# Gathering pass 0 of a mixture-of-experts stage straight from the fp32 residual

## The reference

```python
x = x + gt1[:, None, :] * (merged @ w_o[l])
h2 = modulate(rmsnorm(x, norm2_g[l]), sh2, sc2)
x = x + gt2[:, None, :] * hier_moe(h2, rg_w[l], rg_b[l], re_w[l], re_b[l], exp_w1[l], exp_w3[l], exp_w2[l])
...
(jax.nn.silu(xblk @ w1[e]) * (xblk @ w3[e])) @ w2[e]
```

## Time and profile before

| | |
|---|---|
| median of 3 runs | 1790.93 us (1787.37 to 1791.93) |
| profiled execution, its own time | 1790.77 us |
| its span, first to last instruction | 1789.0 us |
| PE busy | 1741.2 us (97%) |
| DVE, ACT busy | 892.9 us, 393.7 us |
| read from HBM | 639 MB |

### The profile page before, as it was taken

How to read it: one execution, slowest core, us unless ns; L and a number is a source line. 1 busy time by engine, 2 the same in 40 slices (tenths; PEclk the granted TensorE clock), 3 DMA queues, 4 the chain that set the end, 5 groups by cost and what they waited for, 6 DMA issues and landing times.

```text
span 1789.0 us, 25919 instructions
## 1 busy us (share of the span) xinstructions
PE 1741.2 (97%) x10198; PEld 993.7 (56%) x10198; DVE 892.9 (50%) x1032; ACT 393.7 (22%) x480; POOL 0.8 (0%) x5
## 2 busy tenths in 40 slices
PE   4999999999999999999999999999999999999997
PEld 3888567777777776874434444444444444444442
DVE  5564959867778678555233323232323333333334
ACT  3001034433333233434111111110101010101011
POOL 0000000000000000000000000000000000000000
PEclk9999999999999999999999999999999999999999
DMA  9998539889879697654999999999999999999996
GB/s 368 387 379 323 188 142 344 331 310 353 331 290 363 244 371 305 238 201 188 408 422 422 422 422 422 422 422 422 422 422 422 422 422 422 422 422 422 422 422 272
DMA packets 137583, 641.95 MB, mean 359 GB/s; under 512 B 9155, under 2 KB 9283, under 8 KB 77251
## 3 DMA queue, kind: packets, MB, share of 16 engines
q1 hardware_dynamic: 137106, 639.18, 89.4%
q0 software_dynamic: 144, 1.70, 0.2%
q10 hardware_dynamic: 290, 0.46, 0.1%
HBM read 639.21 MB, written 2.10 MB: 358 GB/s over the span
## 4 chain that ended last, share of the span: by engine, by line
PE 78%; DMA 18%; DVE 2%; issue 1%; ACT 1%; SPq 0%; DVEq 0%; ACTq 0%
PE ps L951 18%; DMA ring<-in_exp_w 17%; PE ps L593 8%; PE ps L905 7%; PE ps L688 7%; PE ps L690 7%; PE ps L689 6%; PE ps L650 5%; PE ps L928 4%; PE ps L883 4%; PE ps L606 3%; PE ps L763 2%; PE ps L761 2%; PE ps L762 2%; DMA r_b<-in_ada_w 1%; PE ps L892 1%
## 5 line engine op out<-in xcount | busy, mean ns | idle before, releaser
L951 PE MATMUL ps<-ring 128*64 128x512 f32 x2048 | 466.3, 597 | 5.1 <-DMA ring<-in_exp_w 5.1
L951 PEld LDWEIGHTS ps<-ring 128*64 128x64 f32 x2048 | 143.3, 137 | 292.0 <-issue 291.9
L1729 DVE TENSOR_TENSOR r_h<-r_h,ps 128x1024 f32<-128x1024 f32 x124 | 146.0, 1218 | 204.4 <-PE ps L928 204.4
L689 PE MATMUL ps<-g_lo,h_hi 128*128 128x512 f32 x512 | 199.3, 389 | 0.0
L1702 DVE TENSOR_TENSOR r_c<-ps,scale 128x512 f32<-128x512 f32 x64 | 44.1, 689 | 284.0 <-PE ps L883 282.1
L1274 ACT ACTIVATE r_m<-ps 128x512 f32<-128x512 f32 x32 | 19.1, 597 | 698.6 <-PE ps L951 698.6
L688 PE MATMUL ps<-mix_hi,h_hi 128*128 128x512 f32 x384 | 156.6, 408 | 0.0
L1137 ACT ACTIVATE mix_hi<-ring 128x1024 fp32r<-128x1024 f32 x96 | 101.5, 1061 | 222.3 <-PE ps L690 222.3
L690 PE MATMUL ps<-mix_hi,h_lo 128*128 128x512 f32 x384 | 149.7, 390 | 0.0
L593 PE MATMUL ps<-r_h,ring 128*128 128x256 f32 x640 | 141.9, 385 | 1.3 <-ACT r_h L1083 1.3
L1455 DVE SCALAR_TENSOR_TENSOR r_m<-ring,col,r_m 128x2048 f32<-128x2048 f32 x53 | 124.4, 2347 | 30.3 <-DMA ring<-in_ada_w 30.1
(11 more groups left out here) (271 smaller groups left out, 1621.6 us busy)
## 6 DMA issues: line engine op xcount, KB each, us to landing
ring<-in_exp_w SPq DMA_DIRECT2D x320, 1024.0 KB, 19.9
ring<-in_ada_w SPq DMA_DIRECT2D x72, 1024.0 KB, 8.1
ring<-in_w_in SPq DMA_DIRECT2D x36, 2048.0 KB, 10.0
r_b<-in_exp_w SPq DMA_DIRECT2D x64, 1024.0 KB, 21.7
ring<-in_w_in SPq DMA_DIRECT2D x20, 1024.0 KB, 14.2
r_b<-in_ada_w SPq DMA_DIRECT2D x16, 1024.0 KB, 10.7
ring<-in_w_o SPq DMA_DIRECT2D x8, 2048.0 KB, 9.5
ring<-in_branch_w SPq DMA_DIRECT2D x6, 2048.0 KB, 8.6
```

The lines of the kernel that those rows point to most:

```text
L689: mm(ps[:, b + t, :], h, lo[:, cols], start=False, stop=False)
L951: last = mm(ps[m * NWIN:(m + 1) * NWIN, 2, :], xe[:, k, :], chunk(2 * c + m)[:, kk * F:(kk + 1) * F], start=(k == 0), stop=(k == KT - 1))
L1729: V.tensor_tensor(x1n, x1n, ps[:, (6, 4)[b]:(6, 4)[b] + 2, :].rearrange("p b n -> p (b n)"), ALU.add).then_inc(added, 1)
```

## The change

- **x1.** VectorE writes all eight blocks of x1 before it copies the four turned blocks. ScalarE squares two half tiles before its first copy. TensorE does all 32 transposes before the first logit product.
- **Gather of pass 0.** It reads x1 itself in fp32, with a selection `sel_r` that holds the root of each token's norm in place of a one. The selection is built by four operations on both tiles together. The bf16 selection `sel` is made in full after the tables.
- **Split of tile 1.** The pass 0 gather no longer needs it. Its first two quarters keep their place near the router. The other two and all four second rests are in pass 0, after the second half of the gather, and `gate2_row` waits for the low parts of tile 0. The gather for pass 1 goes from after chunk 1 to after chunk 3 of pass 0. ScalarE does two of tile 1's mid parts, then the exponentials, then waits for the gate row, and does the rest of the split behind it.
- **Small matmul pair.** The pair for the starts (L978, L979) goes ahead of the split of tile 1.
- **Head.** Piece 0 of `ada_w` comes as four transfers, one for each of its four rows, with a semaphore each.

```diff
             for n in range(4):
                 for t in range(TT):
                     turn_x1(n, t)
-                if n == 1:
-                    pe.wait_ge(rw_scaled, 1)
-                if n:
-                    for t in range(TT):
-                        logit_part(n - 1, t)
...
+            pe.wait_ge(rw_scaled, 1)
+            for n in range(4):
+                if n == 2:
+                    mm(ps[:, 5, 0:36], ones, cst_k[:, :], start=True, stop=False)
+                    mm(ps[:, 5, 0:36], ones[0:1, :], lrow[0:1, :], start=False, stop=True).then_inc(cst_done, 1)
+                for t in range(TT):
+                    logit_part(n, t)
...
-            first_rest(1, 0, 2)
             pe.wait_ge(cnt_ready, 1)
             mm(ps[:, 0, 128:160], ct[:, 0, :], tri[0:32, 0:32], start=True, stop=True).then_inc(start_done, 1)
-            first_rest(1, 1, 3)
...
             for b in range(2):
                 pe.wait_ge(lo_ready, b + 1)
-                first_rest(1, 2 + b, 4 + b)
-            for b in range(4):
-                second_rest(1, b, 2 + b)
+                first_rest(1, b, 4 + b)
...
                     if not with_second and c == 0:
                         gate2_row()
+                    if not with_second and c == 1:
+                        gather_x1(1)
+                        pe.wait_ge(gt2_saved, 1)
+                        first_rest(1, 2, 6)
+                        first_rest(1, 3, 7)
+                    if not with_second and c == 2:
+                        for b in range(4):
+                            second_rest(1, b, 4 + b)
...
-                    if c == 1 and not last_pass:
+                    if c == (1 if with_second else 3) and not last_pass:
+                        if not with_second:
+                            pe.wait_ge(lo_ready, 8)
...
-            pe.wait_ge(mid_ready, 8)
-            gather_parts((0, 1))
-            pe.wait_ge(lo_ready, 8)
-            gather_parts((2,)).then_inc(gathered, 1)
+            def gather_x1(half):
+                for kk in range(HALF):
+                    k = half * HALF + kk
+                    for t in range(TT):
+                        last = mm(gat[:, kk, :], x1_k[:, t, k // 4, k % 4, :], sel_r[:, t, :], start=(t == 0),
+                                  stop=(t == TT - 1))
+                last.then_inc(gathered, 1)
+            gather_x1(0)
...
-            pe.wait_ge(xe_ready, 1)
-            gather(1, sel)
...
-            one_hot(0, NWIN)
+            step(first_hot(0))
+            step(first_hot(1))
+            step(V.tensor_tensor(sel_r, sel_r, xs[:, 0:TT, :], ALU.add))
+            step(V.tensor_tensor(sel_r, sel_r, b8(stat[:, 6:8], NWIN), ALU.mult))
             v.sem_inc(all_sel, 1)
...
             for n in range(4):
-                save_x1(n, 0)
-                if n:
-                    save_turned(n - 1)
-                save_x1(n, 1)
-            save_turned(3)
+                for t in range(TT):
+                    save_x1(n, t)
+            for n in range(4):
+                save_turned(n)
```

More of the change, by code:

```diff
@@ L160, in build @@
         xs = r_c[:, 2176:2688].rearrange("p (c n) -> p c n", c=HALF)
+        sel_r = r_c[:, 2688:2816].rearrange("p (t n) -> p t n", t=TT)
         junk = r_m[:, 7168:8192]
@@ L180, in ada_count @@
         def ada_count(i):
-            return 32 * sum(j % ADA_FIRST == i % ADA_FIRST and j % 4 != 3 for j in range(i + 1))
+            return 32 * sum(j % ADA_FIRST == i % ADA_FIRST and j % 4 != 3 and j > 0 for j in range(i + 1))
         def head_w(i):
@@ L217, in build @@
         ada_in = [sem(f"ada_in{i}") for i in range(ADA_FIRST)]
+        ada_first = [sem(f"ada_first{i}") for i in range(4)]
         ada_last = [sem(f"ada_last{i}") for i in range(4)]
@@ L386, in load_head @@
                     sp.wait_ge(sq_done, 2)
-                if piece == 3:
+                if piece == 3 or i == 0:
                     for kk in range(4):
                         sp.dma_start(head_ada(i)[:, kk, :, :],
-                                     ada_v[:, 12 + kk, 0:2 * D].rearrange("p (v n) -> p v n", v=2)
-                                     [:, :, part * PART:(part + 1) * PART]).then_inc(ada_last[kk], 16)
+                                     ada_v[:, 4 * piece + kk, 0:2 * D].rearrange("p (v n) -> p v n", v=2)
+                                     [:, :, part * PART:(part + 1) * PART]
+                                     ).then_inc((ada_last if i else ada_first)[kk], 16)
                     return
@@ L934, in gate2_row @@
                 pe.wait_ge(diag2_ready, 1)
+                pe.wait_ge(lo_ready, 4)
                 for b in range(2):
@@ L1229, in _ @@
             A(stat[:, 20:21], keep[:, K_EPS:K_EPS + 1], ACT.Sqrt).then_inc(warm_up, 1)
+            square(0, 0)
+            square(1, 0)
             copy_turned(0)
-            square(0, 0)
             copy_turned(1)
-            square(1, 0)
+            square(0, 1)
             copy_turned(2)
-            square(0, 1)
+            square(1, 1)
+            copy_turned(3)
             root(0)
-            copy_turned(3)
-            square(1, 1)
             root(1)
@@ L1245, in _ @@
                 part_low(0, b, 4 + b)
[L1246 to L1249, removed]
+            for b in range(2):
+                part_mid(1, b, 4 + b)
             act.wait_ge(r_ask, 1)
@@ L1253, in _ @@
             A(rs[:, 8, :], rs[:, 7, :], ACT.Exp).then_inc(r_exp, 1)
+            act.wait_ge(gt2_row, 1)
+            A(gt2row, ps[:, 6:8, :], ACT.Copy).then_inc(gt2_saved, 1)
+            for b in range(2, 4):
+                part_mid(1, b, 4 + b)
+            for b in range(4):
+                part_low(1, b, 4 + b)
             act.wait_ge(table_ready, 1)
@@ L1356, in _ @@
                         v.wait_ge(ada_last[k - 12], 16 * (part + 1))
+                    elif i == 0:
+                        v.wait_ge(ada_first[k], 16)
                     elif k % 4 == 0:
@@ L1749, in _ @@
             v.sem_inc(table_ready, 1)
+            one_hot(0, PAIRS)
+            v.sem_inc(sel_full, 1)
             modulated(0, 1)
-            one_hot(NWIN, PAIRS)
-            v.sem_inc(sel_full, 1)
             v.wait_ge(r_exp, 2)
```

14 lines of the change are left out of this document (9 added, 5 removed).

## The result

The changed kernel takes 1801.74 us (median of 4 runs, 1800.54 to 1803.46), the kernel before 1790.54 us in as many runs beside it (1787.37 to 1791.93). The ratio is 1.0066, with a 95% interval of 1.0048 to 1.0083. So the change made the kernel **slower by 0.66%**, 11.2 us, where no measurable difference was forecast. The profiled execution took 1801.13 us.

A forecast was written before the change was run, and what follows sets the result against it. The DMA queue at 422 GB/s was taken to bound the loop; 7.5 us gained before pass 0, less 8.85 us added inside it, with a fresh queue start, left 0.3 us: 1790.5 us, range 1786.0 to 1794.0.

The forecast's parts named there:

- the price of the fp32 gather: Both pass 0 gathers: 0.114 us per instruction, 3.65 us each for 32; bounds 0.08 and 0.133.
- I take one fall, in one of the two: Ahead of chunk 0 of pass 0 or pass 1: one clock fall; none 1.3 us better, two 1.3 worse.
- Rival 3: From chunk 0 of pass 0: clock stays low through the pass, anchor 9 us back, 1799.8 us; chance 0.05.
- the anchor: Start of the unbroken weight stream, released by chunk 0 of pass 1: 861.15 us before, 860.8 forecast.
- The start price of 2.0 us: DMA queue starting from idle: full-rate stream begins 2.0 us behind the release.
- the sum: All terms: chunk 0 of pass 0 7.5 us earlier, pass 0 8.85 us longer, stream 0.3 us earlier, 1790.5 us.
- x1: Ahead of pass 0: logits ready 3.6 us earlier once VectorE no longer waits for TensorE.
- The wait ahead of the second gather of pass 1: In pass 1, the other half's gather waits for VectorE's modulation: 1.7 us added.
- The selection behind chunk 3: End of pass 0: ScalarE's copy of the next selection comes some 0.45 us after chunk 3.
- The head: Start of kernel: VectorE begins piece 0 1.0 us earlier but waits for piece 2; gain at most 0.16, taken as 0.
- Rival 2: Ahead of the passes: the 7.5 us gained survive, 1783.4 us; chance 0.10, plus 0.04 for a part.
- Rival 4: End of pass 0: selection or low parts arrive much later than chunk 3; 3 us more, 1793.9 us; chance 0.03.

The follow-up runs named there:

- gather_contiguous: Changed kernel, with pass 0's fp32 gather reading its 128 weight columns from a contiguous stretch of x1, not every fourth element: 1790.26 us, ratio 1.0002 to the kernel before.
- weight_step: Separate timing kernel that only copies x: groups of matmuls with weight elements 1, 2 or 4 apart; fp32 at 64 columns 0.111, 0.117, 0.232 us per instruction.
- gather_between: Changed kernel, with the second half's fp32 gather matmuls put one by one between those of chunks 0 and 1 of pass 0: 1811.76 us, ratio 1.0119.
- x1_alone: Kernel before plus only the x1 part (eight blocks ahead of the copies, transposes together, two squares first): 1785.1 us, ratio 0.9974.
- gate_early: Kernel before plus the x1 part, with the second gate's row made right behind the logits, not after chunk 0 of pass 0: 1783.99 us, ratio 0.9962.
- head_alone: Kernel before plus only the head part, piece 0 of ada_w in four transfers with their semaphores: 1791.08 us, ratio 1.0003.
- chunk0_first: Kernel before, with the second half's bf16 gather for pass 0 placed behind chunk 0 of that pass, not ahead of it: 1792.04 us, ratio 1.0008.

## Why the prediction was wrong

**The step that failed is the price of the fp32 gather**: "I take 0.114, as the weights weigh more than the columns". It measured 0.239 us for an instruction in the first gather and 0.235 in the second, outside the bounds of 0.08 and 0.133. Both nearest rows, L1002 and the transposes, have weights whose elements lie side by side. The gather's lie 16 bytes apart, as `x1_k[:, t, k // 4, k % 4, :]` in the diff says. The bf16 gather before also took every fourth element and cost 0.039 each, and this hid that the step matters for fp32. That this is the cause is shown twice: in the kernel (`gather_contiguous`, 0.116) and by itself (`weight_step`, 0.232 against 0.111). It cost 4.0 and 3.9 us more than the terms of 3.65.

The prediction cited the Trainium skill, page "TensorE: Matmul & The Clock Gate", section "LDWEIGHTS (loading the stationary operand)", with columns/1.2 ns, 107 ns for 128. The runs agree with it at step 1 (0.111 us for load and matmul) and not at step 4 (0.232).

**The second miss hangs on it: the clock.** "I take one fall, in one of the two" was meant at 1.3 us. With contiguous weights that held. With the slow loads the clock fell in both gathers and stayed low for nearly 14 and some 7 us. The tables cost 3.01 us in place of 1.65 (825.0 less the gather's predicted end), chunk 0 6.09 in place of 4.86, the rests 4.03 in place of 2.15: 4.5 us together. Rival 3 named this place and sign, at 9 us from the anchor and a chance of 0.05. Its mechanism, an array with little to do between the chunks, is not what happened, so that its time (1799.8) lies near the measured one is luck. The falls came inside the gathers, and chunks 1 to 3 ran at full clock.

The account of 10.6 us at the anchor (865.84 - 855.2): gathers 7.9, clock 4.5, less 1.4 for the first gather's early start (818.33 for 819.7) and some 0.4 from the waits at the end of pass 0.

**What held:**

- *The anchor.* The end goes with chunk 0 of pass 1. After: anchor 12.0 us later, stream 10.15 and span 10.2 later. The start price of 2.0 us from the release (about 869.3) gives 871.3, as the windows show. From that row to the end of the span are 935.2 us before, 933.4 after, 933.5 in `gather_contiguous`, 933.5 in `gather_between` and 937.5 in `x1_alone` and `gate_early`. Before, the counted start of the stream is 7.3 us behind that row, since loads of pass 1 were still running, and after it is 5.5, a fresh start: that is the difference between the first two. The 2.3 us by which `x1_alone` exceeds the kernel before lie in the last pass. Its chunk 0, in `x1_alone` and in the kernel before:

```profile
1735.37 5.69 PE L949 MATMUL ps<-ring 128*64 128x512 f32 x16
```

```profile
1740.65 3.65 PE L951 MATMUL ps<-ring 128*64 128x512 f32 x16
```

Up to about 1720 us the queue of `x1_alone` is 5.5 us ahead. Then TensorE stands idle for 2.4 us in both, and the clock falls, in `x1_alone` from about 1732.7 to 1739.5, under this chunk, and before from 1736.4 to 1739.8, ahead of it. So the time from the anchor to the end is fixed but for the last pass, where the chain that ends last runs over VectorE and TensorE and not over the queue. The profiled execution of `x1_alone`, 1787.54 us, is the slowest of its nine.
- *With the right price the sum was right.* `gather_contiguous` has the gather at the assumed price and one fall of the clock. It gave chunk 0 of pass 0 at 824.84 (825.0 predicted), that of pass 1 at 855.00 (855.2), and 1790.26 us (1790.5). That it is right to 0.2 us has some luck in it, since where an execution comes out of the head alone moves it by more.
- *x1.* 3.6 us predicted, 4.06 in `x1_alone`. The 5.10 of the changed kernel hold 0.87 that its execution brought from the head, where the clock fell later (see `head_alone`).
- *The wait ahead of the second gather of pass 1*: 1.7 predicted, 1.51 measured. *The selection behind chunk 3*, 0.45 predicted: the gather for pass 1 (L883) starts right behind the chunk, at 860.03, so nothing.
- *The head*: nothing predicted, nothing measured that is clear of the noise.
- *Rival 2*, that the time gained ahead of the passes survives, fell for the whole change. For `x1_alone`, which adds nothing to pass 0, the gain survives: 5.6 us at the anchor, 4.9 in the time. But it does so through the anchor, and not through the first release that the rival named, as `chunk0_first` shows.
- *Rival 4* fell: neither the low parts nor the selection made anything wait.

The forecast priced the parts only in one sum. The x1 part alone gains 0.26%, and the gather, even at the assumed price, spends that again in pass 0.

## What to carry to other kernels

Before a matmul moves from bf16 to fp32 operands, look at the step between the elements of its weights, and take its price only from a row with the same type and the same step; where there is none, lay the weights out side by side. Find the one release from which a saturated queue runs unbroken, and count every microsecond that is put ahead of it, also inside the first pass, since time gained before that pass is easily spent within it. A change of several parts is worth timing part by part: here one part gained 4.9 us and the others together cost more than three times as much.

## What was not expected of the hardware

- fp32 weights with elements 16 bytes apart cost 0.232 us for each instruction with up to 128 moving columns, 0.111 side by side, 0.117 at 8 bytes; under 512 columns the difference is hidden (0.429).
- The clock fell to 1.2 GHz in each of the four stretches of such loads with 64 columns (two in the changed kernel, one in `gather_between`, one in `weight_step`), though PE shows as busy throughout, and the loads came no slower for it. It did not fall in 14 us of the same matmuls at step 1.
- A matmul on half of the array's columns cost 0.44 us next to its like and 1.00 us between full-width ones with weights 16 bytes apart.
- Where the clock falls in the head differed from execution to execution. Those with the early fall (36.1 to 36.6 us) came out of the head last, up to 2 us behind the others.
